# Block one of a two-block kernel in another order: loads from one queue by use, filters beside the modulation, queries ahead of the context keys

## The reference, cut to what matters

```python
mx = (silu(c) @ w_mod + b_mod);  mc = silu(c_ctx) @ w_mod + b_mod      # 12 slices of 512 columns
sh1, sc1, g1, sh2, sc2, g2 = split(mx, 6)
hc = modulate(rms_norm(ctx, norm1_g), csh1, csc1);  kc, vc = keys and values of hc
spec = hyena_spectrum(...)       # two sine layers, a 64x1024 product, decay, sum of |h|, Fourier transform
hx = modulate(rms_norm(x, norm1_g), sh1, sc1)
p = hx @ w_in                    # q, k, v, three hyena inputs, one Fourier input, three gates of 1024
att = attention(rope(q), [rope(k), kc], [v, vc])                        # 8 query heads, 2 key heads
hy = g2 * long_conv(g1 * long_conv(short_conv(v)))                      # two orders, one spectrum each
fn = real(fft2(u))
m = sigmoid(ga) * (att @ wa) + sigmoid(gh) * (hy @ wh) + sigmoid(gf) * (fn @ wf)
x = x + g1 * (m @ w_out)
x = x + g2 * expert_choice_moe(modulate(rms_norm(x), sh2, sc2))         # 16 experts, 384 MB of weights
```

## Time and profile before

| | us |
|---|---|
| median of 3 runs | 2513.4 (2512.44 to 2513.77) |
| profiled execution, its own time | 2519.87 |
| its span, first to last instruction | 2518.5 |
| up to the first branch product (L715) | 351.97 |
| PE busy over the span | 2088.2 |

### The profile page before, as it was taken

The page is one execution under the profiler, slowest core; times in us unless marked ns, Lnnn a source line. Parts: engine busy times, 40 slices in busy tenths (PEclk is TensorE's granted clock), DMA queues, the critical chain, the costliest instruction groups (busy, mean ns, idle before and its releaser), DMA issues.

```text
span 2518.5 us, 29160 instructions
## 1 busy us (share of the span) xinstructions
PE 2088.2 (83%) x12336; PEld 1394.0 (55%) x12336; DVE 972.3 (39%) x1212; ACT 642.1 (25%) x767; POOL 62.5 (2%) x147
## 2 busy tenths in 40 slices
PE   5789798867667666666668999999999999999998
PEld 3557685211111111111114899777998999777997
DVE  2653433100000000000000665775657665775656
ACT  3222120000000000000000444454445444354444
POOL 0000000000000000000000000100000000100000
PEclk8798898887776777777779999999999999999999
DMA  7224455899999999999999555315555455315552
GB/s 275 99 91 152 159 201 217 365 421 421 421 421 421 421 421 421 421 421 421 421 421 410 177 197 178 107 66 192 193 184 190 138 193 176 125 52 194 197 189 94
DMA packets 93258, 647.43 MB, mean 257 GB/s; under 512 B 11495, under 2 KB 12424, under 8 KB 16328
## 3 DMA queue, kind: packets, MB, share of 16 engines
q1 hardware_dynamic: 89856, 639.93, 65.1%
q10 hardware_dynamic: 3272, 5.64, 0.7%
HBM read 644.48 MB, written 1.05 MB: 256 GB/s over the span
## 4 chain that ended last, share of the span: by engine, by line
PE 50%; DMA 33%; DVE 10%; ACT 3%; issue 2%; POOL 1%; ACTq 1%; SPq 1%; DVEq 0%; POOLq 0%
PE PS L377 12%; PE PS L378 12%; PE PS L379 12%; DMA ring<-in_md 8%; DMA ring<-in_mu 7%; DMA XT<-in_mu 2%; DMA mix<-in_mu 2%; DMA XT<-in_md 2%; DVE low L1681 2%; PE PS L821 2%; DMA HRI<-in_mu 1%; PE PS L787 1%; DMA QT<-in_mu 1%; DMA tables<-in_mu 1%; DMA c_dft<-in_mu 1%
## 5 line engine op out<-in xcount | busy, mean ns | idle before, releaser
L1681 DVE TENSOR_TENSOR low<-ring,WH 128x2048 fp32r<-128x2048 f32 (+1 forms) x164 | 374.4, 2283 | 188.3 <-ACT WH L2038 185.8
L377 PE MATMUL PS<-XH,WH 128*128 128x256 f32 x1408 | 398.7, 283 | 4.5 <-DVE XL L1699 4.5
L378 PE MATMUL PS<-XL,WH 128*128 128x256 f32 x1408 | 398.9, 283 | 0.0
L379 PE MATMUL PS<-XH,low 128*128 128x256 f32 x1408 | 398.1, 283 | 0.0
L2038 ACT ACTIVATE WH<-ring 128x2048 fp32r<-128x2048 f32 (+1 forms) x164 | 313.2, 1910 | 25.6 <-DMA ring<-in_fg 19.9
L377 PEld LDWEIGHTS PS<-XH,WH 128*128 128x128 f32 x1408 | 268.3, 191 | 7.4 <-issue 6.1
L379 PEld LDWEIGHTS PS<-XH,low 128*128 128x128 f32 x1408 | 267.9, 190 | 0.0
L378 PEld LDWEIGHTS PS<-XL,WH 128*128 128x128 f32 x1408 | 266.9, 190 | 1.4
L1663 DVE TENSOR_TENSOR SS<-SS,PS 128x512 f32<-128x512 f32 x16 | 11.0, 688 | 553.0 <-PE PS L787 553.0
L787 PE MATMUL PS<-ring,big 128*32 128x512 f32 x928 | 158.3, 784 | 60.3 <-DMA ring<-in_mu 38.2
L2311 ACT ACTIVATE SS<-PS 128x512 f32<-128x512 f32 x16 | 9.6, 597 | 550.5 <-PE PS L787 550.4
(11 more groups left out here) (395 smaller groups left out, 2997.1 us busy)
## 6 DMA issues: line engine op xcount, KB each, us to landing
ring<-in_mu SPq DMA_DIRECT2D x62, 1024.0 KB, 26.5
ring<-in_md SPq DMA_DIRECT2D x60, 1024.0 KB, 27.0
ring<-in_mg SPq DMA_DIRECT2D x54, 1024.0 KB, 26.7
ring<-in_fg SPq DMA_DIRECT2D x44, 1024.0 KB, 4.9
ring<-in_fu SPq DMA_DIRECT2D x44, 1024.0 KB, 4.9
ring<-in_fd SPq DMA_DIRECT2D x44, 1024.0 KB, 4.9
ring<-in_wmod SPq DMA_DIRECT2D x24, 1024.0 KB, 5.5
XT<-in_mg SPq DMA_DIRECT2D x21, 1024.0 KB, 26.6
```

Of the source, the lines that this page charges most:

```text
L377: t.matmul(o, l[0], r[0], start=start, stop=False, skip_group_check=True)
L378: t.matmul(o, l[0], r[1], start=False, stop=False, skip_group_check=True)
L379: return t.matmul(o, l[1], r[0], start=False, stop=stop, skip_group_check=True)
L1681: own(v.tensor_tensor(low[:, w.slot.index, 0:size], w.flat, WH[:, w.slot.index, 0:size].bitcast(f32), ALU.subtract).then_inc(*c.wl.up()), ...
```

## The change

- **Loads.** Every load of block one comes from SP, in one list by first use (`const` now appends to `queue`). The 25 constants are joined into fewer: `base` (identity, selectors, biases, norm gains, taps), `filt`, `middle` (head gains, rope tables, `selb`, hyena biases, router, iota) and `late`. ACT issues no load.
- **Modulation** slices run in the order of `MODS`: 2, 3 (scale), then 0, 1 (shift), each pair of halves of x^T affined as its shift is there. The two sine layers of the filters (`filter_in`) stand between them. x^T goes to `XT1` (the memory of `gB`), and the keys and values of x are computed in halves of k.
- **Queries** come ahead of ctx; the filter's last layer, its absolute sum and the ctx transposes stand between the query halves; the keys and values of ctx come behind them.
- **Heads.** Query heads are normed and rotated for both row halves at once, with the gain multiplied into the rope tables (`gained`); so are all key heads. `why` 0 and 1 are computed around the transposes of the query heads, and `why` 2, the whole Fourier input and the three turns move into attention's steps. The 12 idle matmuls of `turn_over(2, 12)` are gone.
- **Side work** is one generator, `beside()`: the hyena taps, the four spectrum products, then the gates with the turn of a modulation slice behind the first quarter of the next gate, in a PSUM bank of its own (6 or 7).
- **Behind attention** the spectrum product comes first, the att transposes and the Fourier mix fill the time until it is evicted, and 3, 4 and 3 steps of side work stand between the stages of the convolution.
- The sigmoids of four gates run earlier on ACT; block two's rope tables are computed by DVE and ACT in experts 4 to 6.

```diff
+MODS = (2, 3, 0, 1, 4, 5, 6, 7, 8, 9, 10, 11)
...
+        const(c2T[:, :, :], "c2T", l_c2T)
+        load_mod(0)
+        const(base[:, :], "base", l_id)
+        const(XR[:, :, :], "x_t", l_x)
+        load_mod(1)
+        const(filt[:, :], "filt", l_filt)
+        load_mod(2)
         slots = cycle[0:4]
-        for n in range(4):
-            load_mod(n)
         load("wkv", 0, c.kv, 4)
+        load_mod(3)
+        const(ctx_t, "ctx_t", l_ctx)
...
+            mod_products(0)
+            mod_turn(0)
+            filter_in(0)
...
+            mod_products(1)
+            mod_turn(1)
+            filter_in(1)
+            mod_products(2)
+            mod_turn(2)
+            for m in range(2):
+                keys_values(0, XT1, m, range(4))
+            mod_products(3)
+            mod_turn(3)
+            for m in range(2):
+                keys_values(0, XT1, m, range(4, 8))
+            q_half(0, 0)
+            filter_out(0)
+            context_rows(0)
+            context_rows(1)
...
+            filter_sum(3)
...
+            for q in range(2):
+                quarter("why", 0, 7, q)
             P.wait_ge(c.qn, 2)
...
-            filt, side, filtering = filters(), beside2(), True
-            step(8)
-            step(2)
-            step(4)
-            step(2)
-            turn_over(2, 12)
             P.wait_ge(c.kn, 1)
...
+            spectrum(0)
...
+            step()
+            inverse(0)
...
+            step(3)
+            spectrum(1)
+            step(4)
+            inverse(1)
+            step(3)
```

More of the change, by code:

```diff
@@ L285, in program @@
         for i in range(2):
-            cycle[4 + i].first = early[16 + i].used
+            cycle[4 + i].last = early[16 + i]
         slots = slots[0:2] + cycle[4:5] + slots[2:3] + cycle[5:6] + slots[3:4]
@@ L436, in hyena, with quarter @@
-            def hyena(n):
-                yield from feature_rows("why", n, 7)
-                yield 1
+                take(m)
+                w = early_parts("wq", h)
+                for k in range(4 * h, 4 * h + 4):
+                    i = mm3(PS[:, m, :], [x[:, k, m * 128:m * 128 + 128] for x in (XTH, XTL)],
+                            [x[:, k % 4, :] for x in w], k == 0, k == 7)
+                i.then_inc(*c.q.up())
+            def quarter(name, n, b, q):
+                take(b)
+                w, i = early_parts(name, n), q // 2
+                for k in range(4 * (q % 2), 4 * (q % 2) + 4):
+                    x = mm3(PS[:, b, i * 256:i * 256 + 256], [y[:, k, i * 128:i * 128 + 128] for y in w],
+                            [XTH[:, k, :], XTL[:, k, :]], k == 0, k == 7)
+                if q == 3:
+                    x.then_inc(*(c.hy if name == "why" else c.gt).up())
@@ L439, in hyena, with hyena_turn @@
+            def hyena_turn(n, b):
                 P.wait_ge(c.hyv, n + 1)
@@ new lines, in hyena_turn, with fourier_quarter @@
+                held[b] = [(c.u, n + 1)]
+            def fourier_quarter(q):
+                take(6)
+                w, m = early_parts("wfn", 0), q // 2
+                for k in range(4 * (q % 2), 4 * (q % 2) + 4):
+                    x = mm3(PS[:, 6, m * 256:m * 256 + 256], [y[:, k, m * 128:m * 128 + 128] for y in (XTH, XTL)],
+                            [y[:, k, :] for y in w], k == 0, k == 7)
+                if q == 3:
+                    x.then_inc(*c.fn.up())
+                    held[6] = [(c.fx, 1)]
@@ L555, in keys_values, with context_rows @@
                     x.then_inc(*c.kv.up())
-            keys_values(0, XT)
-            side = q_work()
-            for j in range(4):
+            def context_rows(j):
                 b = 2 + j % 2
@@ L1291, in hyena @@
-                yield 1
-                yield 1
-            def gate(n):
-                for i in range(4):
-                    if n < 11 and i == (2 if n < 8 else 0):
-                        part()
-                    yield 1
+                k, o = 2 * n + i, HS[:, n % 2, i, :]
+                own(v.tensor_scalar(o, HP[:, i, 0:256], swT[:, k, 0:1], swT[:, k, 3:4], ALU.mult, ALU.add))
+                own(v.scalar_tensor_tensor(o, HP[:, i, 1:257], swT[:, k, 1:2], o, ALU.mult, ALU.add))
```

1047 lines of the change are left out of this document (498 added, 549 removed).

## The result

| | before | after |
|---|---|---|
| median of 4 runs each, same chip | 2512.92 (2507.82 to 2513.77) | 2446.53 (2445.44 to 2451.02) |
| profiled execution, its own time | 2519.87 | 2445.44 |
| first product | 16.75 | 6.22 |
| first query product | 56.21 | 52.19 |
| first scores | 142.77 | 102.99 |

Page of after: span, and GB/s in 40 slices.

The account below looks back on a forecast made before the run. The experts' weight stream bounds the kernel, so time won ahead of the first branch product counts fully: 48 + 57 + 201.6 = 306.6 for 351.97, a gain of 45.4, giving 2468.0 us against 2513.4; range 2450 to 2490.

Parts of the forecast that it names:

- up to the queries: Start to first query product: at 48 us instead of 56.21, 8 us won; ends 44.5 and 54.
- queries to attention: First query product to first scores: 57 us instead of 86.6, from 40.5 of work plus waits and clock.
- attention to first branch product: First scores to first branch product: 201.6 us instead of 209.2, though 11.5 us more work stands in it.
- 12.8 are left: Attention to first branch product: idle time kept from the 27.0 us of before, once waits of 9.0 and 5.2 go.
- so 15.8 idle: Attention to first branch product: 12.8 us kept plus 3 new idle; lost clock scaled from 19.1 to 11.2 us.
- the two largest rows of PE's waits: Behind first scores: 9.0 us for DVE's complex product and 5.2 for the spectra, both forecast to go.
- the waits ahead of 31 us overlap the stream: Opening: reason for putting the queries at 48 us, nearer the load bound of 44.5 than the late end of 54.
- 44.5 at the earliest: Opening: earliest start of the queries, in us, from the fourth modulation pair's landing at 31 plus the operations behind it.
- ACT's free start: Opening: ACT without DMA issues starts at once, first modulation tiles there near 8 us, where PE's first product waited until 16.75.
- Gate tiles bound the side work: Rival, side work in attention: 3 us uncovered on eight gate tiles costs 24 us, leaving a gain of 21; chance 0.12.
- The opening at the lower clock: Rival, opening: all 23.5 us of work at half speed takes 18.7 us more, leaving a gain of 27; chance 0.06.
- Better than the sum: Rival, whole stretch: all waits at their low ends and the clock up throughout, gain 60 to 73 us; chance 0.08.

Follow-up runs that it names:

- experiment 2: Changed kernel with each modulation tile turned right behind its products and side work sharing banks 6 and 7 by turns; 2466.92 us, ratio 0.9816.
- experiment 3: Changed kernel with each modulation tile turned right behind its products, but modulation in bank 6 and gate tiles in bank 7; 2449.40 us, ratio 0.9757.
- both old orders: Changed kernel with early turn and shared banks 6 and 7, plus the order of before behind attention's last value product; 2467.75 us, ratio 0.9826.
- 10 to 12: Changed kernel with another order in the opening: first try 2446.74 us; squares of ctx ahead of second filter sine 2438.40; that plus reciprocal behind rotation 2433.39.
- experiment 8: Kernel before, with ACT's function of c moved ahead of its last 10 constant loads; 2509.30 us, ratio 0.9986.
- (7): Changed kernel with loads of constants, x and ctx issued by ACT ahead of its first function again; 2448.20 us, ratio 0.9753.
- experiment 9: Changed kernel with DVE's reciprocal of the filter sums placed behind the query rotation instead of ahead of it; 2440.04 us, ratio 0.9719.
- the combined kernel: Changed kernel with the new opening order (squares of ctx ahead of second filter sine) and the reciprocal behind the query rotation; 2433.39 us, ratio 0.9693.

## Why the prediction was wrong

The three steps, and what the trace has for them (to 287.61):

| step | forecast | after | off |
|---|---|---|---|
| up to the queries | 48 | 52.2 | +4.2 |
| queries to attention | 57 | 50.8 | -6.2 |
| attention to first branch product | 201.6 | 184.6 | -17.0 |

**The step that failed is the sum of the third: "12.8 are left", "so 15.8 idle, and lost clock in proportion, 19.1 x 15.8/27.0 = 11.2".** The work was right: 174.6 forecast, 172.5 measured. The losses were 27.0 forecast and 12.1 measured. Of the 14.9 us between, 7.2 are idle time and 7.7 lost clock. Two things were wrong in it.

First, I took out the two largest rows of PE's waits and kept the rest as a lump, without asking for each what makes it wait. A good part of the rest had a cause that the change names: the gate tiles took banks 6 and 7 by turns, with the modulation slices always in 7, and now each has its own while both run. Experiments 2 and 3 show it: the shared bank alone is worth 21.4 us in this stage. In the trace of before three rows are of this kind, 6.1 of the 12.8 us:

```profile
PE PS L393 <- ACT big L2038: 2.7, 2, 2.3
PE PS L377 <- DVE gB L1269: 2.4, 2, 1.6
PE PS L377 <- DVE modT L1264: 1.0, 1, 1.0
```

The first is a modulation product that waits for a gate tile's eviction, the other two are gate products that wait for a slice's addition; in experiment 2 the same three kinds come to 9.5 us, in experiment 3 no row of these kinds reaches 0.6. The other 6.7 were not tried one by one. The Trainium skill, "Perfetto Trace Analysis", Matmuls, says that independent groups should rotate through different PSUM banks, so that the eviction of one overlaps the products of the next. The runs agree as to the overlap, with the addition that rotating is of no use where it leads into the bank of another group: in 2 the gate tiles rotate into the modulation's bank, and each waits for the other's eviction or addition; in 3 both stay where they are, and neither waits.

Second, lost clock didn't follow idle time in proportion. I used 19.1/27.0 = 0.71 us of lost clock per idle us. The same quotient is 3.0/8.9 = 0.34 at most for one added gap (by its median it cost no clock at all), 9.0/7.6 = 1.2 for four, 12.4/9.0 = 1.4 for the shared bank (2 less 3) and 3.5/8.6 = 0.41 in what is left of the changed kernel. In these runs many small waits were the dear ones, and these were the ones I had kept. The Trainium skill has this in "TensorE: Matmul & The Clock Gate", A second HAM failure mode: psum-queue depth-cycling: short pauses between matmul groups that cycle through banks can make the clock fall and rise, and the throughput suffers though most products are at full speed. The runs of this case agree: clock 0.92 with shared banks, 0.98 without.

With both old orders put back the losses are 37.2, and 46.1 before. The 9 us between were not tried one by one; the wait of 5.2 for the spectra, which the forecast had taken out rightly, stays at 1.4 in all of these runs and is the largest row by its size.

**Up to the queries (+4.2).** The load bound was read rightly: x landed at 11.33 (forecast 11) and the fourth pair of modulation tiles at 30.62 (forecast 31). From that pair's products to the queries it took 12.1 us, where the forecast had 13.5. What failed is the step between, that the products would follow the landing closely ("the waits ahead of 31 us overlap the stream"). They came at 40.12, 9.5 us behind it:

```profile
4.29 14.12 DMA filt<-in_filt
...
33.55 6.63 PE PS L547 x16
40.19 1.90 PE PS L413 x16
```

PE stood 5.2 us for `filt`, since the first sine layer was put ahead of the transposes of x, and DVE did the sine layers ahead of the next slice; then the first half of the keys and values (6.63, at a clock of 0.65) stood ahead of the fourth pair. The other order (10 to 12) has its products at 32.8 and starts the queries at 44.2 to 44.7, which is the forecast's "44.5 at the earliest", and there the loads are the bound. The gain from ACT's free start didn't come as such: an earlier first product is used up at the next norm (8), and a later one costs nothing (7). The 4.0 us that were won over before come by exclusion from the order of modulation, keys and ctx; no run shows that part alone.

**Queries to attention (-6.2).** Work 31.15 x 0.99 + 14.38 x 0.80 = 42.3 (40.5 forecast). The rotation's wait is 4.7 (4.5 forecast), and experiment 9 shows that it and the clock behind it are on the path. Idle time is 5.3 in all, for 12.5: the 6 us for filter products that wait for an eviction and the 2 for the key heads came to 0.6. Lost clock is 3.2, for 4. What took the filter products' waits away was not tried by itself. (By its own working the forecast's ends for this step are 48.8 and 65, not 48 and 66; nothing hangs on it.)

**Behind the first branch product.** 2444.1 - 287.77 = 2156.3, 10.2 less than the 2166.5 of before. That is not the change: from the first expert product (445.47 before, 381.48 after) to the end the fourteen profiled executions take 2059.9 to 2073.0 us. The 2073.0 is that of before; the execution of experiment 8, the same code there, takes 2065.9, among the others. So the 10.2 are mostly the scatter of single executions. The medians show 66.4, of which 64.2 were won ahead of the branch products.

**The rivals.** "Gate tiles bound the side work": in the stage no wait of PE is over 1.8 us, so it didn't happen. "The opening at the lower clock": 0.89 there, where before had 0.83. "Better than the sum", to which I gave 0.08, is what came: not all waits at their low ends, since the opening was over its forecast, but nearly all of the losses behind the scores gone, with the clock at 0.98 there. Its chance was too low because the forecast's own losses were a remainder with no cause, and a remainder can go as a whole.

## What to carry to other kernels

Before you keep a remainder of small waits in a forecast, name the releaser and the PSUM bank of each: here giving two interleaved streams a bank each took out a large part of them. Don't price lost clock in proportion to idle time: here many short waits cost more than one long one. And an early start is worth nothing until the chain behind it, engine by engine, is free to use it; read which operation or landing stands ahead of the next link on PE, DVE and ACT. Where the loads go through a ring, an order that uses tiles sooner also lets the next loads start sooner.

## What the runs showed of the hardware

Four gaps of at most 3.7 us, 7.6 us of idle time in all, cost 9.0 us of lost clock, and one of 8.1 us (8.9 idle) cost 3.0; each figure is from one profiled execution. The medians of 4 runs have the same order (2461.4 and 2453.2, with 2446.5 without gaps), but leave the one gap no lost clock beyond its length. The query transposes took 250 ns each at the lower level behind a wait of 4.7 us (16 in 4.01 us) and 133 ns in the combined kernel, where that wait was gone (8 in 1.06 us, below); in experiment 9 removing it brought the first scores forward by 6.7. A reciprocal of 128x512 on DVE took 3.37 us and a copy of 64x512 0.69.

```profile
75.76 3.37 DVE big L1479
...
79.89 1.06 PE PS L618 x8
```
